# A fp32 transformer kernel's passages between stages done in two halves of 256 tokens

## What is computed

```python
def rms_norm(x, g):
    xf = x.astype(jnp.float32)
    y = xf * lax.rsqrt(jnp.mean(xf * xf, axis=-1, keepdims=True) + RMS_EPS)
    return (y * g.astype(jnp.float32)).astype(x.dtype)
...
        h = h + rms_norm(y, mix_norm_post[layer])
        f = swiglu(rms_norm(h, ffn_norm_pre[layer]), ffn_w_gate_up[layer], ffn_w_down[layer])
        h = h + rms_norm(f, ffn_norm_post[layer])
```

## Time and profile before

| | |
|---|---|
| median of 3 runs | 2199.39 us (2197.33 to 2199.87) |
| the profiled execution | 2198.08 us, its span 2195.9 us |
| TensorE's granted clock in it, mean | 0.983 of full |
| products of 512 tokens or 256 (PE), instructions | 10181 |
| HBM read | 181 MB |

### The profile page before, as it was taken

How to read it: one execution, slowest core, us unless ns; L and a number is a source line. 1 busy time by engine, 2 the same in 40 slices (tenths; PEclk the granted TensorE clock), 3 DMA queues, 4 the chain that set the end, 5 groups by cost and what they waited for, 6 DMA issues and landing times.

```text
span 2195.9 us, 25960 instructions
## 1 busy us (share of the span) xinstructions
PE 2096.7 (95%) x10181; PEld 1724.3 (79%) x10181; DVE 1179.0 (54%) x1975; ACT 707.8 (32%) x1040; POOL 9.7 (0%) x23
## 2 busy tenths in 40 slices
PE   7999999999999999999997999999998799999997
PEld 5887888888788797787876788888786577888885
DVE  5646544422775757747555844432489656444324
ACT  4224322211523323333233522221343554222212
POOL 0000000000000000000000000000000000000000
PEclk9999999999999999999988999999999899999998
DMA  4762222222124151141411222232222112222221
GB/s 166 112 109 77 96 96 96 96 96 96 60 98 131 58 148 64 58 134 58 135 39 39 77 96 96 96 104 98 96 86 77 39 61 94 96 96 96 99 101 49
DMA packets 35914, 198.53 MB, mean 90 GB/s; under 512 B 3912, under 2 KB 4457, under 8 KB 14457
## 3 DMA queue, kind: packets, MB, share of 16 engines
q1 hardware_dynamic: 28248, 182.13, 23.8%
q10 hardware_dynamic: 6656, 12.58, 2.7%
q0 software_dynamic: 928, 2.70, 2.5%
HBM read 181.14 MB, written 3.67 MB: 84 GB/s over the span
## 4 chain that ended last, share of the span: by engine, by line
PE 85%; DVE 8%; ACT 4%; issue 2%; DMA 0%; SPq 0%; DVEq 0%; ACTq 0%
PE bank L1373 78%; PE bank L1596 2%; ACT w_hi L474 2%; DVE c L1249 2%; PE bank L1558 1%; PE bank L1574 1%; DVE w_lo L804 1%; DVE w_lo L802 1%; DVE p L1100 0%; DVE work L857 0%; DVE h L862 0%; ACT p L600 0%; PE bank L1746 0%; DVE v1s L1071 0%; DVE work L878 0%
## 5 line engine op out<-in xcount | busy, mean ns | idle before, releaser
L1373 PE MATMUL bank<-x_hi,w_hi 128*128 128x512 f32 x1760 | 700.7, 398 | 19.5 <-DVE x_lo L815 15.9
L1373 PE MATMUL bank<-x_hi,w_lo 128*128 128x512 f32 x1760 | 687.7, 391 | 0.0
L1373 PE MATMUL bank<-x_lo,w_hi 128*128 128x512 f32 x1760 | 687.2, 390 | 0.0
L802 DVE TENSOR_TENSOR w_lo<-w_raw,w_hi 128x2048 fp32r<-128x2048 f32 x131 | 299.7, 2291 | 469.6 <-ACT w_hi L474 469.6
L1373 PEld LDWEIGHTS bank<-x_hi,w_hi 128*128 128x128 f32 x1760 | 331.6, 188 | 101.1 <-issue 29.7
L1373 PEld LDWEIGHTS bank<-x_hi,w_lo 128*128 128x128 f32 x1760 | 331.5, 188 | 70.8
L1373 PEld LDWEIGHTS bank<-x_lo,w_hi 128*128 128x128 f32 x1760 | 331.9, 189 | 67.1 <-issue 1.4
L474 ACT ACTIVATE w_hi<-w_raw 128x2048 fp32r<-128x2048 f32 x131 | 249.8, 1907 | 375.8 <-PE bank L1373 375.8
L1373 PE MATMUL bank<-ff_hi,w_hi 128*128 (+1 forms) x528 | 205.8, 390 | 4.1 <-DVE work L878 4.1
L1373 PE MATMUL bank<-ff_hi,w_lo 128*128 (+1 forms) x528 | 205.4, 389 | 0.0
L1373 PE MATMUL bank<-ff_lo,w_hi 128*128 (+1 forms) x528 | 205.4, 389 | 0.0
(11 more groups left out here) (189 smaller groups left out, 2055.8 us busy)
## 6 DMA issues: line engine op xcount, KB each, us to landing
w_raw<-w_all SPq DMA_DIRECT2D x167, 1024.0 KB, 4.9
qk<-qk_next ACTq DMA_DIRECT2D x32, 384.0 KB, 10.6
w_raw<-w_all SPq DMA_DIRECT2D x8, 256.0 KB, 6.4
h<-x_t SPq DMA_DIRECT2D x4, 512.0 KB, 7.2
out_t<-h SPq DMA_DIRECT2D x8, 256.0 KB, 2.0
skew<-erow POOLq DMA_DIRECT2D x8, 192.0 KB, 8.7
bias<-skew POOLq DMA_DIRECT2D x8, 128.0 KB, 3.4
pos_i<-pos SPq DMA_DIRECT2D x1, 256.0 KB
```

Of the source, the lines that this page charges most:

```text
L802: ins = v.tensor_tensor(w_lo[p][:, part], w_raw[p][:, part], hi, ALU.subtract)
L1373: ins = mm(out, b if flip else a, a if flip else b, start=start and n == 0, stop=stop and n == 2, **kw)
```

## The change

- The 512 tokens are done in two halves of 256 (`tokens(hf)`) from the last unit of a stage to the third unit of the next. PE finishes all 8 last blocks for half 0, then for half 1; the statistic product of half 0 (`y_stat`) stands behind two blocks of half 1, that of half 1 inside the next stage's first half.
- At t = 1, 2, 4, 6 ACT squares half 1 straight from PSUM and copies it to y itself; at t = 3 and 5 (Y_PARTS) DVE still does.
- The next stage is entered with three units: half 0 of units last + 1 and last + 2, with the third (last + 3) behind block 5; then half 1 of the two; xstat; half 1 of the third.
- A third pair of weight buffers (w_hi2, w_lo2) holds unit last + 1, so that it is split ahead of the transition. last + 2 is rounded at the transition's start, last + 3 in its middle.
- The 30 products are gone. The function table is loaded earlier. The column of r_pre at QKV is made behind the sixth unit. The output leaves in 16 pieces.

```diff
-WARM = 30
...
+HALF_S = S // 2
+Y_ORDER = [None] + [list(range(KC)) if t == 5 else [4, 5, 6, 7, 0, 1, 2, 3] for t in range(1, 7)]
+Y_PARTS = (3, 5)
+def tokens(hf):
+    return slice(hf * HALF_S, (hf + 1) * HALF_S)
+def slot(u):
+    stages = sum(u >= last + 2 for last in LAST_ROWS[1:])
+    return 2 if u - 1 in LAST_ROWS[1:] else (u + stages) % 2
...
+        w_hi.append(sb("w_hi2", [P, UNIT], F32R, at=region + 54272))
+        w_lo.append(sb("w_lo2", [P, UNIT], F32R, at=region + 54272 + UNIT * 4))
...
-            for m in range(KC):
-                sp.wait_ge(h_ready, KC * 5 + m + 1)
-                sp.dma_start(out_t[m], h[:, m, :]).then_inc(out_written, 16)
-            sp.wait_ge(out_written, 16 * KC)
+            for hf in range(2):
+                for m in range(KC):
+                    sp.wait_ge(h_ready, h_count(6, hf, m))
+                    sp.dma_start(out_t[m][:, tokens(hf)], h[:, m, tokens(hf)]).then_inc(out_written, 16)
+            sp.wait_ge(out_written, 16 * 2 * KC)
...
+                if u in LAST_ROWS[1:]:
+                    act.wait_ge(unit_done, u - 1)
+                elif u - 1 in LAST_ROWS[1:]:
+                    if u == FFN_A:
+                        act.wait_ge(mix_ready, KC)
+                elif u - 2 in LAST_ROWS[1:] or u - 3 in LAST_ROWS[1:]:
+                    act.wait_ge(unit_done, u - 2)
+                elif u >= 2:
                     act.wait_ge(unit_done, run(i, per, u - 1))
...
-            def post_norm(t):
...
-                if LAST_ROWS[t] + 2 < UNITS:
-                    round_unit(LAST_ROWS[t] + 2)
-                nc.scalar.preload_act_table_set("natural_log_exp_and_others")
-                act.wait_ge(ystat_done, t)
-                rstd(bank[0][:], work[:, RQ, :], D, yr_ready)
...
+            def y_square(t, hf, i):
+                c, m = tokens(hf), Y_ORDER[t][i]
+                if hf == 0 or t in Y_PARTS:
+                    act.wait_ge(y_copied[hf], copied_count(t, i))
+                    seen = y[:, m, c]
+                else:
+                    if i < KC - 1:
+                        act.wait_ge(y_done, y_count(t, hf, i))
+                    else:
+                        act.wait_ge(unit_done, LAST_ROWS[t] + 1)
+                    seen = bank[m][:, c]
+                if i >= 3:
+                    act.wait_ge(yacc_done, yacc_count(t, hf, i - 2))
+                dst = work[:, ACC if i == 0 else 1 + i % 2, c]
+                nc.scalar.activation(dst, seen, ACT.Square).then_inc(ysq_done, 1)
+                if hf and t not in Y_PARTS:
+                    nc.scalar.activation(y[:, m, c], seen, ACT.Copy).then_inc(y_copied[1], 1)
+            def y_rstd(t, hf):
+                act.wait_ge(ystat_done, 2 * (t - 1) + hf + 1)
+                rstd(bank[3 if hf else 4][:, tokens(hf)], work[:, RQ, tokens(hf)], D, yr_ready)
...
+            def transition(t):
+                last = LAST_ROWS[t]
+                if t < 6:
+                    round_unit(last + 2)
                 for m in range(KC):
-                    act.wait_ge(h_ready, KC * (t - 1) + m + 1)
-                    pre_norm_block(t, m)
-                pre_norm_rstd(t)
+                    y_square(t, 0, m)
+                for m in range(3):
+                    y_square(t, 1, m)
+                y_rstd(t, 0)
+                for m in range(3, KC):
+                    y_square(t, 1, m)
+                    if t < 6:
+                        x_half(t, 0, m - 3)
+                if t == 6:
+                    y_rstd(t, 1)
+                else:
+                    round_unit(last + 3)
+                    x_half(t, 0, 5)
+                    y_rstd(t, 1)
+                    for m in (6, 7):
+                        x_half(t, 0, m)
+                    for m in range(KC):
+                        x_half(t, 1, m)
+                    x_rstd(t)
...
             def down(u0):
+                nc.scalar.preload_act_table_set("natural_log_exp_and_others")
...
+                elif n == FILL_B + 5:
+                    round_unit(FFN_B)
...
+            def residual(t, hf, m):
+                c = tokens(hf)
+                if m == 0:
+                    dve.wait_ge(yr_ready, 2 * (t - 1) + hf + 1)
+                order.link(v.scalar_tensor_tensor(work[:, TMP + m % 2, c], y[:, m, c], gain(POST_GAIN[t] + m),
+                                                  work[:, RQ, c], ALU.mult, ALU.mult))
+                v.tensor_tensor(h[:, m, c], h[:, m, c], work[:, TMP + m % 2, c], ALU.add).then_inc(h_ready, 1)
+            def transition(t):
                 for m in range(KC):
...
-                if last + 2 < UNITS:
-                    rest_unit(last + 1)
-                    rest_unit(last + 2)
-                dve.wait_ge(yr_ready, t)
-            def transition(t):
-                post_norm(t)
+                    y_copy(t, 0, m)
+                    y_add(t, 0, m - 1)
+                if t < 6:
+                    rest_unit(LAST_ROWS[t] + 2)
+                for m in range(3):
+                    y_copy(t, 1, m)
+                    y_add(t, 1, m - 1)
                 for m in range(KC):
-                    residual(t, m)
-                    if t < 6 and m >= 2:
-                        xlo(t, m - 1)
-                        xadd(t, m - 2)
+                    residual(t, 0, m)
+                    if m + 3 < KC:
+                        y_copy(t, 1, m + 3)
+                        y_add(t, 1, m + 2)
+                    if t < 6 and m >= 1:
+                        xlo(t, m - 1, 0, tokens(0))
+                        xadd(t, m - 2, 0, tokens(0))
+                    if t < 6 and m == 5:
+                        rest_unit(LAST_ROWS[t] + 3)
...
+                    xadd(t, KC - 1, 0, tokens(0))
+                for m in range(KC):
+                    residual(t, 1, m)
+                    if t < 6 and m >= 1:
+                        xlo(t, m - 1, 1, tokens(1))
+                        xadd(t, m - 2, 1, tokens(1))
...
+                if u0 + 11 < UNITS:
+                    rest_unit(u0 + 11)
...
+                    dve.wait_ge(rcol_ps, 1)
+                    v.tensor_copy(r_col[:], bank[0][:, 0:8]).then_inc(rcol_ready, 1)
+                    dve.wait_ge(rcol_ready, 1)
...
+                    elif m == 5:
+                        rest_unit(FFN_B)
...
+            def y_stat(t, hf):
+                c = tokens(hf)
+                b = bank[3 if hf else 4]
+                pe.wait_ge(y_copied[1], copied_count(t, KC - 1 if hf else 0))
+                pe.wait_ge(yacc_done, yacc_count(t, hf, 6))
+                mm(b[:, c], ones[:], work[:, 0, c], start=True, stop=False)
+                pe.wait_ge(ysq_done, ysq_count(t, hf, KC - 1))
+                mm(b[:, c], ones[:], work[:, 2, c], start=False, stop=True).then_inc(ystat_done, 1)
             def first_units(t, u):
+                def chunk(hf, l, k):
+                    for m in range(2):
+                        ins = block_of(u + l, m, banks_of(l), [k], tokens(hf))
+                    if hf and k == KC - 1:
+                        ins.then_inc(unit_done, 1)
+                pe.wait_ge(w_split, u + 2)
+                for hf in range(2):
+                    if hf == 0:
+                        pe.wait_ge(y_copied[1], copied_count(t, 3))
+                    for k in range(KC):
+                        pe.wait_ge(x_ready, x_count(t, hf, k))
+                        for l in range(2):
+                            chunk(hf, l, k)
+                        if hf == 0 and k == 3:
+                            y_stat(t, 1)
+                        elif hf == 0 and k >= 5:
+                            if k == 5:
+                                pe.wait_ge(w_split, u + 3)
+                            for third in ((0, 1, 2, 3), (4, 5), (6, 7))[k - 5]:
+                                chunk(0, 2, third)
+                xstat(t)
+                for k in range(KC):
+                    chunk(1, 2, k)
...
-                    for _ in range(WARM):
-                        mm(bank[1][:, 0:3 * P], ident_b[:], mask_b[:], start=True, stop=True)
-                    pe.wait_ge(w_split, u + 2)
...
+                for hf in range(2):
+                    s = tokens(hf)
+                    for i, m in enumerate(Y_ORDER[t]):
+                        if hf:
+                            pe.wait_ge(y_copied[0], copied_count(t, i))
+                        for kk in range(2):
+                            n = 2 * c + kk
+                            ins = products(bank[banks[m]][:, s], weights(u, kk * D + m * P), hi[:, n, s], lo[:, n, s],
+                                           fresh and kk == 0, kk == 1, skip_group_check=hf == 1)
+                        if (hf, i) < (1, KC - 1):
+                            ins.then_inc(y_done, 1)
+                        else:
+                            ins.then_inc(unit_done, 1)
+                        if (hf, i) == (1, 1):
+                            y_stat(t, 0)
+                if t == 6:
```

(47 more changed lines are left out.)

200 lines of the change are left out of this document (82 added, 118 removed).

## The result

The changed kernel takes **2247.18 us** (median of 4 runs, 2244.24 to 2248.86) against 2198.55 (4 runs): 1.022 times the time, 95% interval 1.0202 to 1.0237. It is slower, by 48.6 us. (The changed kernel's profile is of the fastest of its four executions.)

The account below looks back on a forecast made before the run. TensorE, busy 95% of the span, was taken to bound the kernel, so only its idle stretches could give time. 2198.1 us plus 37.8 for the transitions and work between them plus 12 for clock falls gave 2248, range 2216 to 2264.

Parts of the forecast that it names:

- the exit: Before a stage's fourth unit: TensorE idles 4.5 us in transition 1, 9.9 in QKV, for weights rounded after the next norm.
- block 5 held up by the third unit: In the next stage's first half: block 5 queues behind the third unit's weight work; TensorE loses 2.5 us in transition 1.
- the clock behind such waits: Half clock after six long TensorE waits, five exits and block 5 of transition 2: +12 us, bounds 0 and 14.
- Transition 1: Mixer's last unit to fourth unit of the first feed-forward stage: 58.3 us against 54.1, +4.2.
- The gap's gain: Between the mixer's last unit and the feed-forward's first products: 1.3 of 9.06 us left, plus 0.5 at y_stat, -7.3.
- Halves: Split products in the transitions: two of 256 columns cost 0.0127 us more than one whole, 2.4 per transition.
- Transitions 3 to 5: Passages into FFN_B, IN2 and FFN_C, last unit to fourth new unit: +7.7, +5.1 and +7.7 us.
- Transition 2: Passage into QKV, last unit to fourth new unit: 67.1 us against 60.4, +6.7, with clock +2.0.
- The tiny products and the fall behind them: Sixteen products for a column of norms, moved behind QKV's sixth unit: 3.0 us and a clock fall of 1.5.
- The end: Transition 6, last unit's start to last h: second y_stat waits for VectorE's sum, +0.5 us at most, 0.4 taken.
- Warm-up: 0: In the gaps: the warm-up products gave no time directly, so removing them counts 0.
- The faster rival: Exit wait hidden if fourth unit's weights split within 6.6 us of xstat; a transition keeps 3.2; 2180 us, chance 0.08.

Follow-up runs that it names:

- the first run: The changed kernel with each stage's fourth new unit rounded before the next norm's logarithm and its remainder subtracted before the first scaling: 2224.94 us.
- fifth: The changed kernel with the third new unit's weights rounded and split in four quarters between blocks instead of in one piece ahead of block 5: 2228.34 us.
- run 2: The changed kernel with bf16 filler products in each exit wait (25 in the feed-forwards, 57 in QKV, 29 in IN2): 2240.59 us.
- run 6: The changed kernel with quartered third unit, early fourth unit and, at transitions 3 and 5, one copy ahead of the subtraction: 2198.35 us.
- run 7: The kernel before, whole-token norms and warm-up kept, with the third weight buffer, early weight work, earlier table loads and later IN2 memset: 2190.67 us.
- the fourth run: The kernel before with 768 products of the last and first two new units each made as two of 256 columns: 2207.05 us.
- run 3: The kernel before without its 30 warm-up products in each of the five gaps: 2207.89 us.
- runs 6 and 8: run 6; and run 6 with the whole third unit behind the statistic in QKV and IN2, IN2's fourth unit back behind the first gate: 2190.7 us.

## Why the prediction was right

Forecast 2248 (2216 to 2264), measured 2247.2. The causes that it named, the exit, block 5 held up by the third unit, and the clock behind such waits, are what the first, fifth and second runs undo, and with the first two of them undone the whole 48.8 us come back (run 6). That the sum meets the measurement within 1 us is luck: two errors cancel. Without the clock it had +37.8, and the profiles show 30.1; for the clock it had +12, and they show 16.5. The profiles' difference also holds 2.1 in the attention that the change did not make.

- **Transition 1, step by step.** Predicted and traced, from the last unit's start: factor of the first norm 11.2 and 10.6, block 0 at 14.2 and 13.65, rounding of the third unit done at 21.9 and 21.3, block 5 at 25.6 and 24.9, second statistic 47.2 and 46.8, end of the third unit 53.8 and 53.4, fourth unit 58.3 and 57.7. All are 0.4 to 0.7 early, none out of place.
- **The exit.** 4.5 predicted, 4.32 traced in the three feed-forwards; 9.9 and 9.6 in QKV; 5.3 and 5.0 in IN2. The rows of ScalarE above show the order that causes it, and the first run shows it by taking it away.
- **The gap's gain** (-7.3) came: 0.96 us of wait ahead of block 0 instead of 9.06. Without the halves run 7 gets 1.1 of it, 2.8 at transition 2.
- **Halves** at 0.0127 each: 0.011 measured in the fourth run.
- **Transitions 3 to 5** are within 0.6, but partly for the wrong reason: each holds 1.7 of slow clock at block 5 or (transition 5) at the first norm's statistic, which the prediction had at transition 2 alone, and work and waits were shorter than listed by 1.1 to 1.8. Transition 2 came out 1.5 below the forecast.
- **The clock.** The step that failed is "Without the warm-up the entry waits (1.3 to 2.1) are too short for it", with the count of six waits that goes with it. Nine falls came, not six: the three more stand behind waits of 2.19 at block 5 of transitions 3 and 4 and 1.95 at the statistic of transition 5. Where they overlap products they are 3.0 to 5.5 long; half of that, summed over the nine, is 16.5 us against the 12 predicted and the upper bound of 14.
- **Between the stages.** The tiny products and the fall behind them: 4.5 predicted, 2.85 + 1.7 traced. The attention's tail: 1.5 and 0.9. IN2 is longer by 3.0, not by the 2.0 of its fall. The shorter slow stretch in the attention was not foreseen; it varies between the profiles whatever the kernel (6.8 in seven of the other nine, 10.2 and 13.7 in one each), and what sets it stays open.
- **The end** came out 0.4 shorter, not longer.
- **The range's high end** of 2264 is more than its terms give: 2248, 2 more of clock, 0.7 and 0.1 of upper bounds and three falls at 2.0 make 2257.
- **"Warm-up: 0"** holds only together with the gap's end: run 3 puts 9.5 us on it while the gap stands. In the changed kernel it was not tried.
- **The faster rival** named the deciding point: weights of the fourth unit split within 6.6 us of the statistic. Run 1 sets this in the feed-forwards, and with block 5's wait gone too (run 6) transition 1 keeps 3.1, where the rival said 3.2. For the whole kernel it put 2180; runs 6 and 8 gave 2198 and 2191, since in QKV and IN2 it is VectorE's work behind the statistic that ends last.

## What to carry to other kernels

When a serial step is hidden by doing it in halves, the cover has to be counted at both ends: here 66 products became 48 halves behind the second statistic, and an order on another engine that had 3 us to spare became the bound. Try first what of the gain can be had without the halves: run 7 got as far as the best of the mended kernels. Put what TensorE will wait for (a weight split) ahead of what it will not (an activation), and release it in pieces when it has to stand among steps that set the pace. Before crediting a removed wait, read what comes next behind it: of 3.2 us taken off ScalarE's chain only 1.1 was on the path in four of five transitions.

## What the runs showed of the hardware

The clock fell in transitions 2, 3 and 4 behind waits of 2.2 to 4.5 us at block 5, and in transition 5 behind a wait of 1.95 at the statistic, though it held across 2.45 us in the kernel before. Transition 1 of the changed kernel had waits of 0.96 and 2.18 and no fall, transition 4 had 0.96 and 2.19 and a fall. Nor is it the kernel's order alone that tells them apart. With the fillers in the exits (run 2), transition 4 has the same 2.19 us wait at block 5, and the clock holds behind it; at transition 5 it falls there, where the changed kernel's did not. Two windows of run 2, behind block 5 of transitions 4 and 5:

```profile
1622.04:1626.00 3.96, 3.96 (x33) 3.96 (x34) 3.79 (x11) 1.45 (x4) 0.00 (x0) 1.00 0.59 246
1857.10:1860.50 3.40, 3.40 (x16) 3.40 (x17) 3.26 (x9) 1.40 (x4) 0.00 (x0) 0.51 0.72 287
```

What decides was not tried, and each profile is of one execution; a wait of 2 us after other waits can't be taken as safe, nor as a certain loss.
